# A residual held turned for the whole program: two layers and two attention blocks on one core

## The reference, cut to what matters

```python
def rms_norm(x, g):
    xf = x.astype(jnp.float32)
    y = xf * lax.rsqrt(jnp.mean(xf * xf, axis=-1, keepdims=True) + NORM_EPS)
    return (y * g.astype(jnp.float32)).astype(x.dtype)
...
        x = x + merged @ w_merge[l]
        h2 = rms_norm(x, g_ffn[l])
        gt = causal_dwconv(h2 @ w_ffn_gate[l], ffn_conv_w[l])
        x = x + (jax.nn.silu(gt) * (h2 @ w_ffn_up[l])) @ w_ffn_down[l]
```

## Time and profile before

| | |
|---|---|
| Median of 3 runs | 1786.15 us (1782.39 to 1786.66) |
| The profiled execution | span 1784.4 us, first to last instruction; it lies among the three times, so what is around the span is small |
| TensorE matmul (PE) | busy 1726.8 us, 97% |
| VectorE (DVE) | busy 1227.4 us, 69% |
| ScalarE (ACT) | busy 931.5 us, 52% |
| Mean granted TensorE clock | 0.983 |

### The profile page before, as it was taken

One profiled execution on the slowest core, in us unless ns is written; L12 is line 12 of the kernel. 1 busy time (PEld: TensorE's weight loads), 2 busy tenths in 40 slices (PEclk: granted clock), 3 DMA queues, 4 the chain that ended last, 5 costly groups with the idle time before them and its releaser, 6 DMA issues.

```text
span 1784.4 us, 31735 instructions
## 1 busy us (share of the span) xinstructions
PE 1726.8 (97%) x13416; PEld 1631.4 (91%) x13416; DVE 1227.4 (69%) x1927; ACT 931.5 (52%) x1291; POOL 124.5 (7%) x35
## 2 busy tenths in 40 slices
PE   7999999999999999999999998889999999999998
PEld 6998999899989999999999898769998899889986
DVE  6994946798649877567887466877554655666553
ACT  5446655554445545664554355756443665655442
POOL 2620300000004603000000000000000000000000
PEclk9899999999999999999999989999999999999999
DMA  8684546556564654646465555324655476436552
GB/s 231 184 202 131 185 129 218 176 166 204 200 199 138 187 166 142 190 142 212 153 202 191 191 157 154 119 72 148 206 190 197 165 214 169 131 118 204 197 203 71
DMA packets 248636, 305.75 MB, mean 171 GB/s; under 512 B 9266, under 2 KB 223630, under 8 KB 248495
## 3 DMA queue, kind: packets, MB, share of 16 engines
q1 hardware_dynamic: 235959, 289.66, 50.6%
q10 hardware_dynamic: 12536, 14.06, 4.1%
HBM read 299.51 MB, written 4.19 MB: 170 GB/s over the span
## 4 chain that ended last, share of the span: by engine, by line
PE 77%; DVE 14%; DMA 3%; ACT 3%; issue 2%; ACTq 0%; DVEq 0%; SPq 0%
PE psum L477 23%; PE psum L478 23%; PE psum L479 23%; DVE wlo L453 3%; DVE psum L1488 3%; DMA raw<-in_w_in 1%; DVE work L1620 1%; PE psum L2489 1%; DMA work<-in_a_w_v 1%; PE psum L2515 1%; PE psum L2501 1%; DMA raw<-in_b_w_q 1%; DVE work L2288 1%; DVE work L2304 1%; DVE work L1634 1%
## 5 line engine op out<-in xcount | busy, mean ns | idle before, releaser
L445 ACT ACTIVATE whi<-raw 128x2048 fp32r<-128x2048 f32 (+2 forms) x277 | 524.1, 1901 | 366.2 <-PE psum L479 258.5
L453 DVE TENSOR_TENSOR wlo<-raw,whi 128x2048 fp32r<-128x2048 f32 x249 | 567.0, 2282 | 197.0 <-PE psum L479 161.9
L477 PE MATMUL psum<-hT,whi 128*128 128x256 f32 x1890 | 525.3, 278 | 0.0
L478 PE MATMUL psum<-hT,whi 128*128 128x256 f32 x1890 | 524.2, 277 | 0.0
L479 PE MATMUL psum<-hT,wlo 128*128 128x256 f32 x1890 | 523.7, 277 | 0.0
L477 PEld LDWEIGHTS psum<-hT,whi 128*128 128x128 f32 x1890 | 356.3, 189 | 0.0
L479 PEld LDWEIGHTS psum<-hT,wlo 128*128 128x128 f32 x1890 | 356.2, 188 | 0.0
L478 PEld LDWEIGHTS psum<-hT,whi 128*128 128x128 f32 x1890 | 356.1, 188 | 0.0
L453 POOL TENSOR_TENSOR wlo<-raw,whi 128x2048 fp32r<-128x2048 f32 (+1 forms) x28 | 123.3, 4405 | 573.9 <-ACT whi L445 394.9
L477 PE MATMUL psum<-whi,hidden 128*128 128x512 f32 x352 | 137.3, 390 | 1.0 <-issue 1.0
L479 PE MATMUL psum<-whi,hidden 128*128 128x512 f32 x352 | 137.0, 389 | 0.0
(11 more groups left out here) (383 smaller groups left out, 3371.7 us busy)
## 6 DMA issues: line engine op xcount, KB each, us to landing
raw<-in_w_in SPq DMA_DIRECT2D x78, 1024.0 KB, 5.7
raw<-in_ffn_w_up SPq DMA_DIRECT2D x44, 1024.0 KB, 5.1
raw<-in_w_ffn_gate SPq DMA_DIRECT2D x22, 1024.0 KB, 5.3
raw<-in_w_ffn_up SPq DMA_DIRECT2D x22, 1024.0 KB, 5.4
raw<-in_w_ffn_down SPq DMA_DIRECT2D x22, 1024.0 KB, 5.0
raw<-in_ffn_w_down SPq DMA_DIRECT2D x22, 1024.0 KB, 4.9
raw<-in_b_w_q SPq DMA_DIRECT2D x12, 1024.0 KB, 6.3
raw<-in_a_w_in SPq DMA_DIRECT2D x10, 1024.0 KB, 5.4
```

The source lines that it names most:

```text
L445: act.activation(part(whi, n, HIGH_SLOTS), part(raw, n, RAW_SLOTS), ACT.Copy).then_inc(high_made, 1)
L453: eng.tensor_tensor(part(wlo, n, LOW_SLOTS), part(raw, n, RAW_SLOTS), part(whi, n, HIGH_SLOTS).bitcast(F32), ALU.subtract).then_inc(stream ...
L477: nc.tensor.matmul(dst, left[0], right[0], start=first, stop=False)
L478: nc.tensor.matmul(dst, left[0], right[1], start=False, stop=False)
```

## The change

`x` is kept as [128 of the width, 8, 256 tokens] from its loading (the host hands it over turned) to the last product but one. `add_rows_product` becomes `add_columns_product` for seven of the eight products: the weight tile stands, the 256 tokens move. The transposes go. Squares are taken tile by tile without a row sum; VectorE adds them over tiles, and a product by a column of ones sums over partitions (`sum_columns`), on TensorE, behind unit 0 of the next stage. The root is made in the next stage, and `spread_root` moves into the middle of unit 1. For the last product `x` is turned back in the last FFN-up stage.

```diff
-        x = sb("x", [P, TT, D])
+        x = sb("x", [P, KT, S])
...
-        def columns_product(pe, b, w, src):
+        def columns_product(pe, b, w, src, root_base=None):
             for j in range(2):
+                if j and root_base is not None:
+                    spread_root(pe, root_base)
...
+        def high_pair(act, dst, gain, b):
+            for k in (2 * b, 2 * b + 1):
+                ins = act.activation(dst[0][:, k, :], x[:, k, :], ACT.Copy, scale=gain(k))
+            ins.then_inc(rows_high.sem, 1)
+        def low_pair(dve, dst, gain, b):
+            dve.wait_ge(rows_high.sem, rows_high.at(b + 1))
+            for k in (2 * b, 2 * b + 1):
+                ins = dve.scalar_tensor_tensor(dst[1][:, k, :], x[:, k, :], gain(k), dst[0][:, k, :].bitcast(F32),
+                                               ALU.mult, ALU.subtract)
+        def square_pair(act, b):
+            act.activation(region(512 * b, 512), pair_of(x, b), ACT.Square).then_inc(rows_squared.sem, 1)
+        def sum_squares(dve):
+            total = region(0, 512)
+            for b in range(1, 4):
+                dve.wait_ge(rows_squared.sem, rows_squared.at(b + 1))
+                v_link(dve.tensor_tensor(total, total, region(512 * b, 512), ALU.add))
+            dve.tensor_tensor(root_diag.rearrange("p t s -> p (t s)"), total[:, 0:S], total[:, S:2 * S], ALU.add) \
+               .then_inc(squares_summed.sem, 1)
+        def sum_columns(pe, base):
+            pe.wait_ge(squares_summed.sem, squares_summed.at(1))
+            for t in range(TT):
+                mm = nc.tensor.matmul(bank((base ^ 4) + 3)[:, t:t + 1], root_diag[:, t, :], cst[:, C_ONE:C_ONE + 1],
+                                      start=True, stop=True)
+            mm.then_inc(columns_summed.sem, 1)
+        def roots_of_rows(dve, base):
+            dve.wait_ge(columns_summed.sem, columns_summed.at(1))
+            inverse_root(dve, root, stat[:, 6:6 + TT], stat[:, 8:8 + TT], bank((base ^ 4) + 3)[:, 0:TT], 1.0 / D, 1)
...
```

`add_columns_product`, the last unit on TensorE, then ScalarE, then VectorE:

```diff
+                        for b in range(4):
+                            for k in range(2):
+                                for m in (2 * b, 2 * b + 1):
+                                    mm = tile(m, k)
+                            mm.then_inc(unit_used.sem, 1)
...
+                make_high(act, n0 + count + 3)
+                act.activation(stat[:, 150:151], cst[:, C_ONE:C_ONE + 1], ACT.Sqrt)
+                for b in range(4):
+                    act.wait_ge(rows_added.sem, rows_added.at(b + 1))
+                    high_pair(act, raw_T[kind], gain, b)
+                    square_pair(act, b)
...
+                make_lows(dve, n0 + count + 2)
+                add(0)
+                for b in range(4):
+                    if b < 3:
+                        add(b + 1)
+                    low_pair(dve, raw_T[kind], gain, b)
+                sum_squares(dve)
+                make_lows(dve, n0 + count + 3)
+                end(dve)
```

The next stage, TensorE behind unit 0, ScalarE and VectorE at their start:

```diff
-                        spread_root(pe, turned)
+                        sum_columns(pe, turned)
...
-                copy_root(act, turned)
                 make_high(act, n0 + 4)
+                root_of_variance(act)
+                copy_root(act, turned)
...
+                roots_of_rows(dve, turned)
                 dve.wait_ge(root_spread.sem, root_spread.at(1))
```

The last FFN-up stage, behind units 6 to 9 (ScalarE copies each bank back to rows of `x`):

```diff
+                        for i in range(4):
+                            mm = nc.tensor.transpose(bank(turned + q)[:, i * P:(i + 1) * P],
+                                                     x[:, 4 * (q % 2) + i, (q // 2) * P:(q // 2 + 1) * P], ident)
```

More of the change, by code:

```diff
@@ L359, in two_part_transformer @@
         final_load = signal("final_load")
-        x_load = [signal(f"x_load{h}") for h in range(2)]
+        x_load = [signal(f"x_load{b}") for b in range(4)]
         angles_ready = signal("angles_ready")
@@ L750, in _ @@
                 nc.tensor.transpose(bank(0)[:, 0:P], early, ident).then_inc(gains_turned.sem, 1)
-                turn_rows(pe, base, [(x_load[h].sem, x_load[h].at(16)) for h in range(2)])
                 end(pe)
@@ L797, in copy_distances, with add_columns_product @@
             dve.wait_ge(side_free.sem, side_free.at(4))
-        def add_rows_product(lhsT, nk, base, kind, gain):
+        def add_columns_product(operand, nk, base, kind, gain):
             n0, count = len(stream.freed), nk // 2
-            total = len(stream.units)
             @block.tensor
@@ L845, in _, with add @@
                 begin(dve)
[L846 to L855 removed]
+                make_lows(dve, n0 + count + 2)
+                def add(b):
+                    dve.wait_ge(unit_used.sem, unit_used.at(count + b))
+                    dve.tensor_tensor(pair_of(x, b), pair_of(x, b), bank(base + b), ALU.add).then_inc(rows_added.sem, 1)
+                add(0)
+                for b in range(4):
+                    if b < 3:
+                        add(b + 1)
+                    low_pair(dve, raw_T[kind], gain, b)
+                sum_squares(dve)
+                make_lows(dve, n0 + count + 3)
                 end(dve)
@@ L859, in add_rows_product, with _ @@
             rows_added.close(4)
-            if kind:
-                close_roots(1)
             close_stage()
             return base ^ 4
-        def ffn_up_stage(conv, turned, gain):
+        x_rows = region(20000, TT, D)
+        def add_rows_product(lhsT, nk, base):
+            n0, count = len(stream.freed), nk // 2
+            @block.tensor
+            def _(pe):
+                for c in range(count):
+                    w = take_unit(pe, n0 + c)
+                    await_pair(pe)
+                    last = c == count - 1
+                    for t in range(TT):
+                        for h in range(2):
+                            for k in range(2):
+                                mm = three_passes(bank(base + 2 * t + h),
+                                                  [v[:, 2 * c + k, t * P:(t + 1) * P] for v in lhsT],
+                                                  [v[:, k, h * 512:(h + 1) * 512] for v in w],
+                                                  c + k == 0, 2 * c + k == nk - 1)
+                            if last:
+                                mm.then_inc(unit_used.sem, 1)
+                    if not last:
+                        mm.then_inc(unit_used.sem, 1)
+                    release_unit(unit_used, c + 1 + 3 * last)
+                end(pe)
+            @block.scalar
+            def _(act):
+                begin(act)
+                act.dma_start(region(18500, D), a["final_norm_2"].partition_broadcast(P)).then_inc(final_load.sem, 16)
+                make_high(act, n0 + count)
+                act.activation(stat[:, 150:151], cst[:, C_ONE:C_ONE + 1], ACT.Sqrt)
+                for q in range(4):
+                    t, h = q // 2, q % 2
+                    act.wait_ge(rows_added.sem, rows_added.at(q + 1))
+                    ins = act.activation(region(512 * q, 512), x_rows[:, t, 512 * h:512 * (h + 1)], ACT.Square,
+                                         accum_out=part_sum[:, 2 * h + t:2 * h + t + 1])
+                ins.then_inc(rows_squared.sem, 1)
+                end(act)
+            @block.vector
+            def _(dve):
+                begin(dve)
+                make_lows(dve, n0 + count)
+                for q in range(4):
+                    xs = x_rows[:, q // 2, 512 * (q % 2):512 * (q % 2 + 1)]
+                    dve.wait_ge(unit_used.sem, unit_used.at(count + q))
+                    dve.tensor_tensor(xs, xs, bank(base + q), ALU.add).then_inc(rows_added.sem, 1)
+                end(dve)
+            unit_used.close(count + 3)
+            rows_added.close(4)
+            close_stage()
@@ L1117, in dense @@
                     for j in range(2):
+                        if n == j == 1:
+                            spread_root(pe, turned)
                         for k in range(KT):
```

181 lines of the change are left out of this document (81 added, 100 removed).

## The result

The changed kernel takes 1829.54 us (median of 4 runs, 1825.97 to 1836.24) against 1784.9 for the kernel before: 44.6 us more, ratio 1.0266, 95% interval 1.0247 to 1.0284. The forecast was 1820.0, range 1802 to 1836. So sign and range held, and the time was 9.5 us too low.

What follows compares the result with a forecast made beforehand. TensorE was taken to bound the kernel, with 77% of the chain. Products 9.0, joints 22.8 and last turn 1.9 us sum to 33.7 on 1786.15: 1820 us, 1.9% slower, range 1802 to 1836 (8 in 10).

Steps and rivals of the forecast that it cites:

- The stall in unit 1: Behind each product, TensorE waits 2.6 us mid-unit 1 for the root, behind VectorE's low part and ScalarE's high part.
- the 0.8 us of waiting ahead of the column sums: After unit 0 of the next stage, TensorE waits about 0.8 us for VectorE's `sum_squares`.
- The products: Seven products split into 256-column matmuls at 117.8 ns: 9.0 us more without their last units, bounds 0 and 10.5.
- a sign of being wrong (more than 118): The forecast would be wrong if the products' 256-column matmuls went at more than 118 ns, or at 113.3.
- the second pace: 256-column matmuls at 117.8 ns, 8.9 ns more per former matmul; chosen because the `ffn_rows` stream began behind a wait.
- The joints of FFNs and dilated attention: Stage changes behind products, later by 7.8 us (two FFNs with convolution), 4.0 (two without) and 2.0 (dilated attention).
- the last turn: 16 transposes in the last FFN, in a stage where TensorE has no gap: 1.9 us more.
- Setup, second mixer, compressed attention: Later by 6 us in setup (between 3 and 8), 2.5 in the second mixer, 0.5 in compressed attention.
- The clock rival: New waits slow TensorE's clock, 1.7 us at each of seven or eight joints: plus 6 to 14 us, 1826 to 1834; chance 0.11.
- The hidden wait: Root made within unit 1's first 2.83 us, so every joint keeps its 0.9 us: 1780 to 1790 us; chance 0.09.
- The fast pace: The products' 256-column matmuls stay at 113.3 ns: 1809 to 1811 us; chance 0.20.

Runs made afterwards that it cites:

- 1: Changed kernel with ScalarE's square root of the variance issued ahead of its high part of unit 3; 1818.11 us, ratio 1.0177.
- 2: Changed kernel with VectorE's low part of unit 2 issued behind the root and its diagonal; 1817.85 us, ratio 1.0185.
- 3: "Both orders": changed kernel with the root issued ahead of ScalarE's high part of unit 3 and VectorE's low part of unit 2; 1806.22 us, ratio 1.0122.
- Experiment 4: Changed kernel with the moving tiles of the seven turned products starting at 448 bytes modulo 512 instead of 128; 1820.89 us, ratio 1.0205.
- 7: Changed kernel with 12 of the 16 transposes that turn the residual back in the last FFN left out; 1827.48 us.
- 5: 3 together with the shifted addresses of Experiment 4; 1798.53 us, ratio 1.0088.
- 6: 3 with the square-root table loaded earlier in setup and compressed attention's two memsets behind its first low parts; 1801.74 us, ratio 1.0118.
- 8: 6 with Experiment 4's addresses, and raw rows of FFN, mixer and dilated stages at 448 bytes modulo 512; 1795.67 us, ratio 1.0076.
- 9: 8 with the raw rows back and the last FFN's hidden tiles at their old address; 1794.86 us, ratio 1.0062.
- 11: 3 with early table, late memsets, shifted addresses, last FFN's hidden tiles at old address, 10's GpSimd low part, mixer's high part of unit 4 earlier; 1800.03 us.
- 10: 3 with unit 3's low part made by GpSimd instead of VectorE in the two FFNs with a convolution; 1814.19 us, ratio 1.0172.

## Why the forecast was right, and by how much it was off

The direction and the mechanism of the stall were right; the time was too low by 9.5 us, and by 16.3 in the profiled execution. Of these the products are 4.0, setup and first mixer 4.1, the second mixer 3.0, compressed attention 4.2 and the rest 1.0. Nearly all of it lies on one side, and the range held because it was wide enough; within the joints one error hid another, as told below.

*The stall in unit 1* was forecast at 2.6 us and measured at 2.5 to 2.7 at all seven joints behind products. Its cause, two transfers in series ahead of the root, is shown by 1, 2 and 3. One part of the working was off without harm: `sum_squares` took 2.6 us instead of 2.9, the 0.8 us of waiting ahead of the column sums did not come, and unit 1 started 0.4 us earlier than forecast (U + 12.4), the root some 0.5 earlier; the wait, a difference of the two, was the same.

*The products*: this step failed. The two paces of the earlier trace rows were taken as the only ones, with 117.8 ns as the upper bound. The products went at 120.0 throughout, which the prediction itself had named as a sign of being wrong (more than 118). Over 1176 former matmuls that is 15.7 us where 10.5 were allowed for at most; without the last units, 13.0 against 9.0. The pace was carried over from `branch` and `ffn_rows` to `joined` as if it belonged to the shape. Experiment 4 shows that it goes by the place: `branch` and `ffn_rows` start at 64 bytes modulo 512, `joined` and `hidden` at 128. The reason given for the second pace, that a stream behind a wait takes it, doesn't hold in the trace before either: unit 0 of the second FFN, behind the same wait, went at 113.3 (39 matmuls from 857.95 to 862.37). The Trainium skill, "TensorE: Matmul & The Clock Gate", section "Back-to-back issue gap", would have 109.2 ns for 256 columns at full clock (an estimate from that page's formula, which it gives for an isolated matmul). No stream of 256 columns here reached it, and the formula has one gap where the runs show three.

*The joints of FFNs and dilated attention*: 14.4 measured against 13.8, and close in each kind, in part by luck. Falls of the clock, which are not in the forecast, cost 1.7 us each in the first FFN without a convolution and in dilated attention. Without them these three joints come to 3.3 us where 6.0 were forecast: unit 2 was late by 1.5 us and not 2.0, and `ffn_rows` went at 113.3 ns where it had gone at 117.8. The like joints without a fall in 4 and 7 took 1.4 to 1.5 us each, without the last turn.

*Setup, second mixer, compressed attention*: 20.3 measured against 9.0, mis-sized. For the setup, the gate was forecast 5.4 to 7.6 us late and came 10.5 late, since the high part ahead of the root waited 4.76 us for its raw unit. The first product came 8.4 to 10.1 us late in the five executions without both orders (the changed kernel, 1, 2, 4, 7). With both it came 0.8 us early to 4.4 late (3, 5, 6, 8, 9, 11), and 8.1 late in 10, which had another wait of 4.9 us in that mixer. So the order costs some 4 to 11 us there. The clock has a share in it that can't be split off: up to the first product it was at 1.2 GHz for 20.5 us before, for 30.7 in the changed kernel and for 17 to 27 with both orders (10 apart).

In the second mixer the clock was at 1.2 GHz from 587.9 to 601.6, 13.7 us, where it was for 6.8 before (569.2 to 576.0). The runs give the price. With both orders the second mixer took 0.4 us less than before with 6.8 us at 1.2 GHz (10), 1.1 to 1.2 more with 10.2 us (3, 6, 8, 11), and 2.9 more with 13.7 us (5, 9). So 3.4 of the 5.5 us are the clock's, and 2.1 are left for the forecast's 2.5.

In compressed attention the prediction had counted that TensorE loses little. ScalarE and VectorE ahead of the root there:

```profile
1079.13 1.92 ACT L448 ACTIVATE whi<-raw 128x2048 fp32r<-128x2048 f32 x1 [5.18 <-DVEq L411]
1079.64 1.76 DVE L2354 MEMSET work<- 128x2048 f32 x1 [0.59 <-DVEq L411]
...
1083.58 0.16 DVE L537 TENSOR_SCALAR stat<-psum 128x2 f32<-128x2 f32 x1
```

The high part runs beside the two fills, as the prediction had it. But the fills, which stood behind the root before, now stand ahead of it in series with the low part, to 1083.54. TensorE waited 2.40 us in unit 1, and a later unit waited 4.3 us where it had waited 2.2 before. With both orders the layer is 1.0 us faster than before.

*The clock rival* (chance 0.11) came true in part: falls behind three of seven stalls, at its price of 1.7 us each, and none behind any of them when the stalls were at 0.9 us or less (1 to 3; the compressed attention's, where the clock is low before the stall, apart). Of the two other kernels with the whole stall, 4 has one such fall and 7 two. The profiled execution was more afflicted than the others: 45.9 us of missing clock against 40 to 44. The Trainium skill, "TensorE: Matmul & The Clock Gate", section "Part 4: PE-mode transpose", says that transposes don't count as busy for the clock in the way that matmuls do. By that the old joints, 2.3 us of transposes and waiting, were about as idle as the new ones; but apart from compressed attention only the new ones show falls. The lengths are too close for the runs to decide on it.

*The hidden wait* did not occur: the sum of the two transfers would have had to be under 1.6 us and was 4.2. *The fast pace* did not occur in the products.

*What remains* of the change's cost once its order is mended and its operands are moved is 0.6%, 11 us by the ratio (9). Its profiled execution starts its last product 13.7 us later than the one before the change. 6.5 of them are in the products, of which two long ones went at 117.8 ns; 4.4 in setup and first mixer; 2.9 in the second mixer, at twice the time at 1.2 GHz; 3.1 in the FFNs with a convolution, with waits of 1.3 us ahead of unit 4 and 0.4 ahead of unit 3; 2.3 for the last transposes. The other stretches are 5.5 shorter. No version beat the kernel before. Not settled: what decides between 113.3 and 117.8 ns when a stream begins, and what sets the time at 1.2 GHz in the mixers.

## What to carry to other kernels

When a computation is moved ahead of a stage's end, list what each engine still issues between the last input and the value that others wait for. Here two transfers that TensorE did not need yet, 2.3 and 1.9 us long, cost 23 us over eight joints, more than the transposes that the change removed had cost (seven times 2.0). A saved instruction is worth what ends last behind it.

And take a matmul's pace only from rows with the same operands at the same addresses; the shape alone left 6% open.

## What the runs showed of the chip that was not expected

- fp32r matmuls of 256 columns at full clock have three paces by address. With the moving and the standing tiles both at 128 bytes modulo 512: 120.0 ns, in every turned product of every kernel left so. With the moving tiles at 448, or at 64 as the raw rows are, and the standing at 128: 113.3 or 117.8 ns, kept by a product from its start. Which of the two differs between the profiled executions of kernels that have this product alike (the third hidden product: 113.3 in 4, 117.8 in 8), and within one execution between stretches of the same tiles; whether it differs between executions of one kernel isn't known. At 512 columns with the standing tiles shifted instead: 233.3 ns against 226.7. That the address sets it is shown; by what means isn't.
- The second mixer did nearly the same work in the seven kernels with both orders. It took 1.5 to 1.8 us more with each further 3.4 us at 1.2 GHz (-0.4, 1.1 to 1.2 and 2.9 us against the kernel before, with 6.8, 10.2 and 13.7 us). So part of what looks like the price of an edit in one execution is the clock's.
- A GpSimd `tensor_tensor` from SBUF and VectorE's with two SBUF inputs stop one another: VectorE's four took 6.09 us for 2.51, ending 2.4 us after GpSimd's. The Trainium skill, "SBUF — State Buffer", section "Who interferes with whom", says that a VectorE instruction with two SBUF inputs contends with a GpSimd instruction that reads SBUF, for ports that one holds while the other blocks, and that one with at most one SBUF input does not. The trace agrees in both halves: 6.09 for L625, 0.68 for L1022.
